# Order of copies, splits and squares in the mixers, and the first w2 in quarters, in a one-core hybrid block

## What is computed

```python
h = _rmsnorm(x, norm_mix)
z = h @ w_in                                   # 2048 x 11296
# mixer A (gated DeltaNet, 8 heads): short causal convolution on q, k, v, then SiLU
qkv = silu(causal_depthwise_conv(concat[aq, ak, av], conv_a))
oa = gated_delta_rule(l2norm(aq), l2norm(ak), av, sigmoid(abeta), g)
ya = (rmsnorm(oa, a_norm) * silu(az)) @ w_oa
# mixer B (GLA, 4 heads): per-channel forget gate, chunked
ob = gla_chunked(bq, bk, bv, gk);  yb = (rmsnorm(ob, b_norm) * silu(bg)) @ w_ob
x = x + (sigmoid(mix_a) * ya + sigmoid(mix_b) * yb) @ w_out
# MoE: top-1 of 4 groups, top-2 of 8 experts in it, 32 SwiGLU experts of width 512
x = x + hier_moe(rmsnorm(x, norm_ffn), w_rg, b_rg, w_re, b_re, w1, w3, w2)
y = rmsnorm(x, norm_final)
```

## Time and profile before

| what | value |
|---|---|
| median of 3 runs | 1803.4 us (1797.27, 1803.4, 5274.58) |
| the profiled execution's own time | 1797.45 us |
| its span | 1795.7 us |
| its mean granted TensorE clock | 0.99 |
| TensorE busy | 1726.4 us (96%) |
| VectorE, ScalarE, GpSimd busy | 675.6, 444.1, 169.6 us |
| HBM read | 534.42 MB, 299 GB/s over the span |

### The profile page before, as it was taken

The page is one execution under the profiler, slowest core; times in us unless marked ns, Lnnn a source line. Parts: engine busy times, 40 slices in busy tenths (PEclk is TensorE's granted clock), DMA queues, the critical chain, the costliest instruction groups (busy, mean ns, idle before and its releaser), DMA issues.

```text
span 1795.7 us, 20998 instructions
## 1 busy us (share of the span) xinstructions
PE 1726.4 (96%) x8774; PEld 1104.3 (61%) x8774; DVE 675.6 (38%) x740; ACT 444.1 (25%) x483; POOL 169.6 (9%) x223
## 2 busy tenths in 40 slices
PE   9999999999999999999999999999999999999996
PEld 7888878888788888888544434443444443443342
DVE  5357767455744645543222202221122112220222
ACT  6344455325523433333100000000000000000002
POOL 4000042310051100000000000000000000000001
PEclk9999999999999999999999999999999999999999
DMA  8454535423533455658999999999999999999997
GB/s 262 145 168 161 164 118 187 141 94 118 171 111 105 137 188 187 225 174 321 369 419 429 427 428 429 428 429 429 428 429 428 429 428 428 428 429 428 428 425 298
DMA packets 95323, 537.41 MB, mean 299 GB/s; under 512 B 5836, under 2 KB 5900, under 8 KB 70044
## 3 DMA queue, kind: packets, MB, share of 16 engines
q1 hardware_dynamic: 94672, 535.85, 75.4%
q0 software_dynamic: 592, 0.69, 0.3%
HBM read 534.42 MB, written 2.10 MB: 299 GB/s over the span
## 4 chain that ended last, share of the span: by engine, by line
PE 72%; DMA 22%; DVE 2%; ACT 2%; issue 1%; POOL 0%; SPq 0%; DVEq 0%; ACTq 0%; POOLq 0%
DMA arena<-in_w 22%; PE psum L1994 13%; PE psum L1532 12%; PE psum L1534 12%; PE psum L1533 12%; PE psum L2021 9%; PE psum L1915 4%; PE psum L1754 1%; PE psum L1746 1%; PE psum L2039 1%; PE psum L2038 1%; PE psum L1646 1%; DVE w_lo L1044 1%; PE psum L1956 1%; PE psum L1757 0%
## 5 line engine op out<-in xcount | busy, mean ns | idle before, releaser
L1994 PE MATMUL psum<-arena 128*64 128x512 f32 x2048 | 458.8, 605 | 39.2 <-DMA arena<-in_w 38.5
L1994 PEld LDWEIGHTS psum<-arena 128*64 128x64 f32 x2048 | 148.1, 139 | 338.9 <-issue 288.0
L1044 DVE TENSOR_TENSOR w_lo<-arena,w_hi 128x2048 fp32r<-128x2048 f32 x119 | 273.2, 2298 | 194.1 <-ACT w_hi L711 184.1
L1532 PE MATMUL psum<-w_hi,hT_hi 128*128 128x512 f32 x824 | 332.1, 403 | 0.1
L1534 PE MATMUL psum<-w_hi,hT_lo 128*128 128x512 f32 x824 | 327.6, 398 | 0.0
L1533 PE MATMUL psum<-w_lo,hT_hi 128*128 128x512 f32 x824 | 327.6, 398 | 0.0
L711 ACT ACTIVATE w_hi<-arena 128x2048 fp32r<-128x2048 f32 x119 | 227.5, 1914 | 258.8 <-PE psum L1534 249.1
L2021 PE MATMUL psum<-arena 128*64 128x512 f32 x960 | 210.6, 594 | 3.4 <-DMA arena<-in_w 3.4
L1534 PEld LDWEIGHTS psum<-w_hi,hT_lo 128*128 128x128 f32 x824 | 155.8, 189 | 37.9
L1532 PEld LDWEIGHTS psum<-w_hi,hT_hi 128*128 128x128 f32 x824 | 156.1, 189 | 36.6 <-issue 0.9
L1533 PEld LDWEIGHTS psum<-w_lo,hT_hi 128*128 128x128 f32 x824 | 156.2, 190 | 35.7
(11 more groups left out here) (365 smaller groups left out, 1409.0 us busy)
## 6 DMA issues: line engine op xcount, KB each, us to landing
arena<-in_w SPq DMA_DIRECT2D x184, 2048.0 KB, 26.4
arena<-in_w_in SPq DMA_DIRECT2D x87, 1024.0 KB, 5.0
arena<-in_w_out SPq DMA_DIRECT2D x16, 1024.0 KB, 5.1
arena<-in_w SPq DMA_DIRECT2D x14, 1024.0 KB, 20.9
arena<-in_w_oa SPq DMA_DIRECT2D x8, 1024.0 KB, 5.0
arena<-in_w_ob SPq DMA_DIRECT2D x8, 1024.0 KB, 5.0
arena<-in_x SPq DMA_DIRECT2D x4, 1024.0 KB, 7.6
arena<-in_w SPq DMA_DIRECT2D x4, 512.0 KB, 15.7
```

The costliest lines, as they stand in the source:

```text
L1044: tt(w_lo[x % RING_A], ringA[:, x % RING_A, :], w_hi[x % NSPLIT].bitcast(F32), ALU.subtract)\
L1532: mm(m_banks[m], lhs[0][:, k0 + k, ms], wh[:, cs], start=(start and k == 0), stop=False)
L1994: i = mm(bank(w)[e * CAP:(e + 1) * CAP, :], xeT[:, k, e * CAP:(e + 1) * CAP], src[e][:, (k % 8) * CB:(k % 8 + 1) * CB], start=(k == 0), st ...
```

## The change

It touches five places.

1. **Copies ahead of splits.** The `zqT` copy on ScalarE, and the `obT0` and `zkT` copies on VectorE, no longer issue the splits that `result` put ahead of them; these come behind.
2. **Squares ahead of the third convolution.** ScalarE takes the decays' Exp first, and the squares of q and k ahead of the third Tanh; VectorE puts SiLU `w - 1` into the convolution `w`, after its tap 1.
3. **First chunks with high parts first.** The matmuls of the first two chunks are ordered so that those with `w_hi` run before those with `w_lo`, and the waits are split likewise.
4. **Small gaps.** `smallT` gets one filler and `blrT` one fewer; the root-mean-square chain on GpSimd has two operations fewer behind its wait; 36 instead of 30 dummy transposes ahead of the ranks, and 6 new ones ahead of the first gather.
5. **First w2 in quarters.** All four w2 slots of the first pair come in halves of 1 MB, in the order of the quarters of w1 that free them.

```diff
@@ SPANS
-    {"small": 1, "smallT": 0, "cw": 1, "blrT": 2, ...
+    {"small": 1, "smallT": 1, "cw": 1, "blrT": 1, ...
@@ SyncE
-            for half in range(2):
+            for t, (freed, name) in enumerate(((("first_part", 2), "part_in"), (("slotM_free", RING_M + 2), "slotM0"),
+                                               (("first_part", 3), "w2_third"), (("slotM_free", RING_M + 4), "slotM1"))):
+                wait(sp, freed)
                 for e in range(2):
-                    if half:
-                        sp.wait_ge(sem("slotM_free"), RING_M + e + 1)
-                    else:
-                        wait(sp, ("first_part", 2))
-                    sp.dma_start(ringM[e][:, half * D:(half + 1) * D], w2_v[e, :, half * D:(half + 1) * D])\
-                        .then_inc(sem("slotM0" if half else "part_in"), 16)
-            load_pair(0, 0, 0, RING_M + 2, PER_PAIR)
+                    sp.dma_start(ringM[2 * (t // 2) + e][:, t % 2 * D:(t % 2 + 1) * D], w2_v[e, :, t * D:(t + 1) * D])\
+                        .then_inc(sem(name), 16)
@@ GpSimd
+                link(nc.gpsimd.tensor_scalar(rqk[:, 0:8], rqk[:, 0:8], QSCALE, None, ALU.mult))
+                link(nc.gpsimd.tensor_tensor(rmf[:, 8:16], rqk[:, 0:8], rqk[:, 0:8], ALU.mult))
                 wait(pool, ("a_ms", g + 1))
-
-                link(nc.gpsimd.tensor_scalar(rqk[:, 0:8], rqk[:, 0:8], QSCALE, None, ALU.mult))
-                link(nc.gpsimd.tensor_tensor(rms[:, 0:8], rms[:, 0:8], rqk[:, 0:8], ALU.mult))
-                link(nc.gpsimd.tensor_tensor(rms[:, 0:8], rms[:, 0:8], rqk[:, 0:8], ALU.mult))
+                link(nc.gpsimd.tensor_tensor(rms[:, 0:8], rms[:, 0:8], rmf[:, 8:16], ALU.mult))
@@ ScalarE
                 for i, w in ((0, "zqT"), (2, "zvT")):
-                    result(w + s)
+                    if i:
+                        sp_.before(w + s)
+                    wait(act, full(w + s))
...
-                for i in range(3):
-                    sp_.before("ssq" + s, most=2 if i else 3)
-                    act.wait_ge(sem("conv"), 3 * g + i + 1)
-                    nc.scalar.activation(T_[f"zT{i}"][:, 0:1024], c[i], ACT.Tanh, scale=0.5).then_inc(sem("tconv"), 1)
...
-                for i in range(2):
-                    act.wait_ge(sem("silu"), 3 * g + i + 1)
-                    nc.scalar.activation(T_[f"zT{i}"][:, 0:1024], c[i], ACT.Square).then_inc(sem("sq"), 1)
+                for i, most in enumerate((3, 2, 1)):
+                    sp_.before("ssq" + s, most=most)
+                    if i == 2:
+                        for j in range(2):
+                            act.wait_ge(sem("silu"), 3 * g + j + 1)
+                            nc.scalar.activation(T_[f"zT{j}"][:, 0:1024], c[j], ACT.Square).then_inc(sem("sq"), 1)
+                        sp_.before("ssq" + s, most=1)
+                    act.wait_ge(sem("conv"), 3 * g + i + 1)
+                    nc.scalar.activation(T_[f"zT{i}"][:, 0:1024], c[i], ACT.Tanh, scale=0.5).then_inc(sem("tconv"), 1)
@@ VectorE
-                if i:
-                    wait(dve, full(f"obT{i}"))
-                else:
-                    result(f"obT{i}")
+                wait(dve, full(f"obT{i}"))
...
-                result("zkT" + s)
+                wait(dve, full("zkT" + s))
...
+                        if w and k == 1:
+                            silu(w - 1)
@@ TensorE
-            keep_running(30)
+            keep_running(36)
...
-                        if first and w == 0 and q == 0:
+                        if first and w == 0 and q % 2 == 0:
                             i.then_inc(sem("first_part"), 1)
...
+            keep_running(6)
             wait(pe, ("first_sel", 1))
```

More of the change, by code:

```diff
@@ L84 @@
 SPANS = [
-    {"small": 1, "smallT": 0, "cw": 1, "blrT": 2, "gc": 1, "gkT": 4, "bkT": 2, "lv_eye": 2, "lv1": 2, "lv2": 1,
+    {"small": 1, "smallT": 1, "cw": 1, "blrT": 1, "gc": 1, "gkT": 4, "bkT": 2, "lv_eye": 2, "lv1": 2, "lv2": 1,
      "lv4": 2, "lv8": 1, "lv16": 2, "lv32": 1, "lv64": 2, "kd": 1, "bo1": 3},
@@ L1232, in _, with silu @@
                 cwv = cw.rearrange("p (w h k) -> p w h k", w=3, h=A_HEADS)
+                def silu(w):
+                    dve.wait_ge(sem("tconv"), 3 * g + w + 1)
+                    stt(c[w], T_[f"zT{w}"][:, 0:1024], 1.0, c[w], ALU.add, ALU.mult).then_inc(sem("silu"), 1)
                 for w in range(3):
@@ L1244, in _ @@
                             link(i)
+                        if w and k == 1:
+                            silu(w - 1)
                     i.then_inc(sem("conv"), 1)
-                for w in range(3):
-                    dve.wait_ge(sem("tconv"), 3 * g + w + 1)
-                    stt(c[w], T_[f"zT{w}"][:, 0:1024], 1.0, c[w], ALU.add, ALU.mult).then_inc(sem("silu"), 1)
+                silu(2)
                 result("ssq" + s)
@@ L1565, in _ @@
             for half in range(2):
+                ks = (2 * half, 2 * half + 1)
+                wait(pe, ("w_hi", 1) if half else ("first_half", 1))
                 for m in range(NM):
+                    ms = slice(m * P, (m + 1) * P)
                     if half == 0:
                         wait(pe, ("hTl", m + 1))
+                    for k in ks:
+                        cs = slice(k * CB, (k + 1) * CB)
+                        mm(bank(m), hTh[:, k, ms], w_hi[0][:, cs], start=(k == 0), stop=False)
+                        mm(bank(m), hTl[:, k, ms], w_hi[0][:, cs], start=False, stop=False)
                     if m == 0:
                         wait(pe, ("w_lo", 1) if half else ("first_half", 2))
-                    for k in (2 * half, 2 * half + 1):
-                        cs, ms = slice(k * CB, (k + 1) * CB), slice(m * P, (m + 1) * P)
-                        mm(bank(m), hTh[:, k, ms], w_hi[0][:, cs], start=(k == 0), stop=False)
-                        mm(bank(m), hTh[:, k, ms], w_lo[0][:, cs], start=False, stop=False)
-                        i = mm(bank(m), hTl[:, k, ms], w_hi[0][:, cs], start=False, stop=False)
+                    for k in ks:
+                        i = mm(bank(m), hTh[:, k, ms], w_lo[0][:, k * CB:(k + 1) * CB], start=False, stop=False)
             i.then_inc(sem("chunk"), 1)
@@ L1579, in _ @@
                     wait(pe, ("hTl", 2 * x + 2))
-                project(x)
+                if x > 1:
+                    project(x)
+                    continue
+                for wait_for, lhs, w in ((("w_hi", 2), hTh, w_hi[1]), (None, hTl, w_hi[1]), (("w_lo", 2), hTh, w_lo[1])):
+                    if wait_for:
+                        wait(pe, wait_for)
+                    for m in range(NM):
+                        for k in range(CT):
+                            i = mm(bank(m), lhs[:, CT + k, m * P:(m + 1) * P], w[:, k * CB:(k + 1) * CB], start=False,
+                                   stop=False)
+                i.then_inc(sem("chunk"), 1)
             wait(pe, ("small_split", 2))
@@ L2013, in expert_pair @@
                     return last_down(n, u, arrived)
-                if first:
-                    wait(pe, ("part_in", 48))
                 for t in range(FT):
-                    if t % 2 == 0:
+                    if first:
+                        wait(pe, (("part_in", 48), ("slotM0", 64), ("w2_third", 32), ("slotM1", 64))[t])
+                        src = ringM[t // 2 * 2:t // 2 * 2 + 2]
+                    elif t % 2 == 0:
                         src = arrived(8 + t)
```

## The result

The changed kernel takes 1810.45 us in the median of 5 runs (1808.6 to 1811.4), the kernel before, with two more runs added, 1798.01 (lowest 1797.27). The ratio is 1.0059, with a 95% interval of 1.0042 to 1.0077, so the changed kernel is slower by 0.6%. The profiled execution's own time is 1810.45 us and its span 1808.7 us, 13.0 more than before. The prediction was 1799.1 us with a range up to 1806: too low by 11 us.

What follows compares the result with a forecast made beforehand. TensorE was taken to pace the kernel up to about 850 us, and DMA of the expert weights behind that. The terms summed to +1.65 us on the profiled 1797.45, giving 1799.1 us, with a range of 1793 to 1806.

Steps and rivals of the forecast that it cites:

- Group 1, +7.2 and +2.2: Start of group 1: moved `zqT` copy delays splits and `oaT.0`'s read-out, +7.2 us; slow clock after the idle time, +2.2.
- Group 0, -0.5: Same copy edit at the start of group 0: nothing blocks, the wait at `gcb` goes, -0.5 us (-1.5 to +0.5).
- The clock at `ssq.1`, -4.8: Squares ahead, group 1: the 1.49 us wait and the slow stretch behind it go, -4.8 us; -1.5 if the clock falls.
- the second rival: Clock falls again at `ssq.1` or stays low longer after the stall: -1.5 instead of -4.8, 1802.4 us; 25%.
- First chunks, -1.1: First two chunks: high parts first shorten TensorE's waits for the low splits, -1.1 us (0 to -1.7).
- Small gaps, +0.3: `smallT` and `blrT`: a filler covers the 0.6 us wait, but later work comes late, +0.3 us (-0.6 to +0.9).
- GpSimd's chain, -0.45: Ahead of `oaT.1`: two short links fewer on GpSimd close the 0.5 us wait, -0.45 us.
- Routing and w2, -1.2: Start of the experts: dummies keep the clock up at the gathers, w2 quarters fill a DMA hole; -1.2 us (0 to -4.5).
- the first (no stall, 1789.7): Rival: the group 1 stall isn't there or is hidden, the 9.4 us fall away and the gains stand, 1789.7 us; 15%.
- the signs named for "wrong": No long wait near 440 to 450; low clock at `ssq.1`; TensorE waiting over 1 us at fillers of `gcb.0` or `gc`.

Runs made afterwards that it cites:

- e3: Changed kernel with ScalarE's `zqT` copy put back behind its splits in group 0 only: 1802.62 us, 1.0007 of the kernel before.
- e4: Changed kernel with ScalarE's `zqT` copy put back behind its splits in group 1 only: 1801.70 us, 1.0006 of the kernel before.
- e13: Changed kernel with two of the three high splits ahead of the `zqT` copy in both groups: 1797.24 us, 0.9977 of the kernel before.
- e11: e5 with the squares part of the change undone (Exp, squares, Tanh and SiLU in the old order): 1792.63 us, 0.9961 of the kernel before.
- e12: The kernel before with only `ssq` split into halves, the first filler chunk between them: 1794.40 us, 0.9969 of the kernel before.
- e7: e2 with the first w2 in its old order, two slots in halves and two whole: 1794.03 us, 0.9953 of the kernel before.
- e14: e5 with the fillers of `smallT` and `blrT` as before: 1789.15 us, 0.9937 of the kernel before.
- e6: e2 with the squares part of the change undone (Exp, squares, Tanh and SiLU in the old order): 1794.68 us, 0.9961 of the kernel before.
- e2: Changed kernel with only ScalarE's `zqT` copy put back behind its splits, in both groups: 1794.49 us, 0.9964 of the kernel before.
- e5: e2 with `ssq` split into halves, the first filler chunk between them: 1788.54 us, 0.9922 of the kernel before.
- e8: e2 with the dummy transposes as before, 30 ahead of the ranks and none ahead of the first gather: 1794.92 us, 0.9951 of the kernel before.
- e9: e5 with the first w2 in its old order, two slots in halves and two whole: 1789.27 us, 0.9941 of the kernel before.
- e10: e5 with the dummy transposes as before, 30 ahead of the ranks and none ahead of the first gather: 1789.64 us, 0.9945 of the kernel before.
- e15: e5 with VectorE's `obT0` and `zkT` copies also back behind their splits: 1790.15 us, 0.9946 of the kernel before.

## Why the prediction was wrong

- **Group 1, +7.2 and +2.2: right.** The wait was 8.71 us for the 8.7 worked out, for the read-out of `oaT.0` and once, and the whole came to +9.03 for 9.4. The read-out let `zkT.1` start 8.21 us later for the 8.2 worked out; from there to the first filler it took 6.18 us (457.06 to 463.24), 2.0 more than the 4.2 at full clock, for the 2.2 taken. That the one copy makes the stall is shown by e3 and e4, that it does so through the low splits by e13.
- **Group 0, -0.5: this is the step that failed.** The prediction said that "nothing blocks", because VectorE has no split ahead of its copies there. It looked at VectorE's queue and at the splits for the fillers of `gcb.0`, and left out what else stands behind the copy on ScalarE: beside three high splits the read-out of v's block, for which `zvT.0` waits. Of a moved step every instruction that now comes later has to be asked who waits for it. It cost +6.66 instead of -0.5, and most of its arithmetic was at hand: three splits of 1.9 us and a read-out like the L726 in the order of ScalarE in group 1. e3 against the changed kernel shows the price, e13 the cause.
- **The clock at `ssq.1`, -4.8: the size was off.** The wait went as forecast, but the slow stretch did not: -1.54, the lower bound given (-1.5), the case that the second rival took at 25%. The term read the slow stretch behind a wait as one that the wait alone had made. Either is enough: the wait ahead of a half block (e11, e12), and the block of 32 one-column matmuls without a wait in 15 of 18 cases. Where the clock did not fall the forecast came true: e7 took 9.2 us from the start of `ssq.1` (489.86) to `ktok.1` (499.06), for the 9.1 worked out. That `ssq` "in group 0 did not bring the clock down" rested on one profiled execution, one of the three exceptions, and in the changed kernel it cost +1.58 there. Both things together, 1.58 and 3.3, are the second half of the miss.
- **First chunks, -1.1: -0.80. Small gaps, +0.3: +0.46. GpSimd's chain, -0.45: -0.55.** Right within their bounds, as read from one profile of each kernel; only the second has a run of its own (e14). The wait ahead of `oaT.1` is gone in e6 too, which keeps the chain and undoes the squares, so it is not the squares that close it. The first matmul is at 10.84 and waits for low tokens (L1056), as described. The loss behind `blrT` came as a wait of 0.94 us at the filler behind `gc`.
- **Routing and w2, -1.2: -2.4.** Inside the bounds, of which the lower, -4.5, left out a third window with idle DMA: 860 to 870 moved 355 GB/s in before. The clock's share of the gathers, forecast at 1.36, was 1.62 (5.46 to 3.84). Behind the first w1 matmul 0.8 more was gained in this pair of profiles, which the quarters are not shown to have made. Besides, no term stood for the 0.55 us lost between `oaT.1` and the end of the chunks, with a wait of 0.3 for L722 there; where the rest of it comes from stays open.
- The sum of what was measured, -0.80 + 0.46 + 6.66 + 1.58 + 9.03 - 1.54 - 0.55 + 0.55 - 1.57 - 0.81 = +13.0, against +1.65. The group 0 term accounts for 7.2 of the 11.4 between them, the clock at the two `ssq` for 4.8, and the rest for -0.6. The sum was laid on the profiled 1797.45, near the fastest of before, whose medians in the later sets are 1800.2 to 1803.1.
- Of the rivals, the first (no stall, 1789.7) is what e2 and e5 made real by moving the copy back: 1794.5, and 1788.5 with the clock kept up. VectorE kept its order: it stood at a blocked split for 10.46 us, the last 3.8 of them with ready work behind it. The Trainium skill, "TensorE: Matmul & The Clock Gate", section "Architectural detail: the array is 16× 32×32, not 1× 128×128", says that ScalarE and VectorE are strict FIFO. By that rule the trace agrees. Of the signs named for "wrong", a low clock at `ssq.1` came. TensorE did not wait at the fillers of `gcb.0`; the stall came ahead of them, at `zvT.0`.

## What to carry over

When an instruction that waits is moved ahead of others on its engine, list everything it passes, and for each of them the one who waits for it: here it was not the splits, whose consumers had slack in group 0, but a read-out at the end of the same list. A copy may pass only as much as the steps behind it can spare: passing the third split and the read-out cost nothing in group 1 and a wait of 2.84 us in group 0. And a slow matmul behind a wait is not yet proof that the wait is the cause; look at the same step in several executions before crediting the clock to an edit. The one profile of before that this prediction had showed the rarer case.

## What the runs showed of the hardware

- TensorE's clock can drop to its lower level (1.2 GHz) with no idle time at all ahead of it. In e2, at `ssq.1`, the engine was busy for all of 485 to 505 us, and the matmuls of the chunk behind took 0.63 us instead of 0.40. What it had been busy with was 32 matmuls of one column. In all profiles together this came in 15 of 18 cases. Two halves of 16 with full matmuls between, 1.84 us each, did it in none of 12, unless a wait of 1.5 us stood ahead (2 of 2). The Trainium skill, "TensorE: Matmul & The Clock Gate", section "What's actually happening", says that the gate goes by how busy the array has been of late, and that it is free-running, so that where in it the work falls varies. The pair e7 and e8, one program up to there and apart behind `ssq.0`, agrees with the second of these. For the first, no run here measures what the gate counts as busy.
- Such falls are a large part of the scatter of this kernel: the runs of before spread over 8.0 and 8.6 us in its two largest sets, those of e12 over 3.4, and those of e5, e9, e10, e14 and e15 over 1.8 to 3.6.
- The lowest median is e5's, the changed kernel with ScalarE's copy behind its splits and `ssq` in halves: 1788.54 us, 0.9922 of before (0.9906 to 0.9939). That is 22 us below the changed kernel's 1810.45. e9, e10, e14 and e15 lie within 1.7 us of it, at 0.9937 to 0.9946, and are not told apart from it.
